# A two-block network on one NeuronCore: modulation panels as blocks, weight and row residuals moved to VectorE, retention's output weights split a head later, and gated attention in pairs of heads

## The reference

```python
def first_block(...):
    h = rms_norm(x, g_mix)
    q, k, v, su, sv, ga, gb = split(h @ w_in)
    y_att = gqa_attention(rope(q), rope(k), v) @ w_att_out     # 8 heads of 64, 2 key/value heads
    y_sgu = spatial_gating(gelu(su), gelu(sv), ...) @ w_sgu_out
    x = x + (sigmoid(ga) * y_att + sigmoid(gb) * y_sgu) @ w_out
    x = x + memory_cross_attention(rms_norm(x, g_cross), mem, w_cq, w_ckv, w_co)   # 4 heads of 128
    x = x + hierarchical_moe(rms_norm(x, g_moe), ...)
    return rms_norm(x, g_final)

def second_block(x, c, ...):
    for i in range(2):
        shift, scale, gate = split(silu(c) @ ada_w[i, 0] + ada_b[i, 0])
        h = x * (1 + scale) + shift
        y = stick_breaking_attention(h, ...) if i == 0 else retention(h, ...)
        x = layer_norm(4 ** 0.25 * x + (1 + gate) * y)
        shift, scale, gate = split(silu(c) @ ada_w[i, 1] + ada_b[i, 1])
        y = grouped_moe(x * (1 + scale) + shift, ...)
        x = layer_norm(4 ** 0.25 * x + (1 + gate) * y)
    return x
```

## Time and profile before

| | us |
|---|---|
| median of 3 runs | 1493.07 |
| lowest, highest | 1492.53, 1499.2 |
| the profiled execution | 1499.87 |
| its span, first to last instruction | 1498.0 |
| mean granted clock of TensorE | 0.975 of full |

### The profile page before, as it was taken

One profiled execution on the slowest core, in us unless ns is written; L12 is line 12 of the kernel. 1 busy time (PEld: TensorE's weight loads), 2 busy tenths in 40 slices (PEclk: granted clock), 3 DMA queues, 4 the chain that ended last, 5 costly groups with the idle time before them and its releaser, 6 DMA issues.

```text
span 1498.0 us, 22670 instructions
## 1 busy us (share of the span) xinstructions
PE 1385.2 (92%) x8222; PEld 862.5 (58%) x8223; DVE 616.9 (41%) x1323; ACT 454.1 (30%) x786; POOL 426.5 (28%) x197
## 2 busy tenths in 40 slices
PE   7999988899999989997899999899998979999985
PEld 6886776544444488775344444498876844444432
DVE  5598444522122243446233333477015254333324
ACT  4554433212121245543111111245435321112101
POOL 6892743100000077051000000279845610000000
PEclk9999999999999999999999999999998989999998
DMA  7664567699999974419699999795525499999951
GB/s 282 221 191 170 184 225 280 276 426 428 428 429 429 410 282 175 170 57 384 248 384 425 430 428 427 276 342 178 204 78 225 138 376 425 385 427 427 428 202 54
DMA packets 89597, 447.62 MB, mean 299 GB/s; under 512 B 7804, under 2 KB 9768, under 8 KB 70952
## 3 DMA queue, kind: packets, MB, share of 16 engines
q1 hardware_dynamic: 85856, 445.87, 74.8%
q10 hardware_dynamic: 3656, 0.57, 0.3%
HBM read 445.38 MB, written 1.05 MB: 298 GB/s over the span
## 4 chain that ended last, share of the span: by engine, by line
PE 66%; DMA 12%; DVE 10%; POOL 5%; issue 3%; ACT 3%; SPq 0%; DVEq 0%; ACTq 0%; POOLq 0%
PE ps L415 62%; DMA ring_hi<-in_w_up 9%; POOL WLO L2383 4%; PE ps L828 1%; PE ps L868 1%; DMA ring_lo<-in_w_co 1%; ACT WHI L1257 1%; PE ps L849 1%; DVE Z L1846 1%; DVE Z L1834 1%; DVE Z L1847 1%; DVE Z L1845 1%; DMA ring_lo<-in_w_ckv 1%; POOL RS L2352 1%; DMA ring_lo<-in_w_out 1%
## 5 line engine op out<-in xcount | busy, mean ns | idle before, releaser
L2383 POOL TENSOR_TENSOR WLO<-ring_lo,WHI 128x1024 fp32r<-128x1024 f32 (+1 forms) x158 | 386.8, 2470 | 686.5 <-ACT WHI L1257 684.7
L415 PE MATMUL ps<-ring_hi,Z 128*64 128x512 f32 x1248 | 280.1, 598 | 8.1 <-DVE Z L2082 3.0
L415 PE MATMUL ps<-ring_lo,Z 128*64 128x512 f32 x1152 | 261.4, 603 | 6.3 <-issue 5.2
L1257 ACT ACTIVATE WHI<-ring_lo 128x1024 fp32r<-128x1024 f32 (+1 forms) x160 | 165.3, 1048 | 217.5 <-PE ps L415 179.7
L415 PEld LDWEIGHTS ps<-ring_hi,Z 128*64 128x64 f32 x1248 | 90.1, 137 | 175.1 <-issue 168.7
L415 PEld LDWEIGHTS ps<-ring_lo,Z 128*64 128x64 f32 x1152 | 83.1, 139 | 159.6 <-issue 159.1
L2085 DVE TENSOR_TENSOR Z<-ps,Z 64x512 f32<-64x512 f32 x50 | 34.7, 694 | 305.1 <-ACT Z L1446 303.3
L415 PE MATMUL ps<-WHI,HTH 128*128 128x512 f32 x320 | 126.9, 397 | 8.9 <-POOL WLO L2383 5.0
L2352 POOL TENSOR_TENSOR RS<-MS,NEGH 128x1 f32<-128x1 f32 (+2 forms) x26 | 22.3, 857 | 370.2 <-DVE MS L1683 309.7
L1446 ACT ACTIVATE Z<-ps 64x512 f32<-64x512 f32 x50 | 29.5, 590 | 322.1 <-PE ps L415 322.1
L415 PE MATMUL ps<-WHI,HTL 128*128 128x512 f32 x320 | 125.2, 391 | 0.0
(11 more groups left out here) (293 smaller groups left out, 1950.3 us busy)
## 6 DMA issues: line engine op xcount, KB each, us to landing
ring_lo<-in_ada_w SPq DMA_DIRECT2D x22, 2048.0 KB, 9.1
ring_lo<-in_moe_w_gate SPq DMA_DIRECT2D x16, 2048.0 KB, 10.3
ring_lo<-in_moe_w_up SPq DMA_DIRECT2D x16, 2048.0 KB, 14.7
ring_lo<-in_moe_w_down SPq DMA_DIRECT2D x16, 2048.0 KB, 13.8
ring_hi<-in_moe_w_gate SPq DMA_DIRECT2D x16, 2048.0 KB, 11.0
ring_hi<-in_moe_w_up SPq DMA_DIRECT2D x16, 2048.0 KB, 15.5
ring_hi<-in_moe_w_down SPq DMA_DIRECT2D x16, 2048.0 KB, 12.8
ring_lo<-in_ret_w_in SPq DMA_DIRECT2D x12, 2048.0 KB, 8.0
```

What stands on the lines that cost most here:

```text
L415: return nc.tensor.matmul(o, l, r, start=start, stop=stop, skip_group_check=True)
L1257: nc.scalar.activation(WHI[:, q, 0:size], slot(r)[:, q * size:(q + 1) * size], Copy).then_inc(S("hi_split"), 1)
L2383: nc.gpsimd.tensor_tensor(WLO[:, q, 0:size], slot(r)[:, q * size:(q + 1) * size], WHI[:, q, 0:size].bitcast(F32), ALU.subtract).then_inc(S ...
```

## The change

Five parts:

1. **Modulation panels.** Panels 6 and 7 leave the cross attention; they are done as one block (`ada_block`, 8 chunks of four groups) behind `co`, panels 8 and 9 as one block in the first routing. Panels 8 and 9 are loaded into `ring_hi`, so all later panels of `ring_lo` take another slot.
2. **Lows on VectorE.** Quarters 0 and 2 of `w_out` 0, quarter 0 of `sb` 2, quarter 0 of `ret` 1, and in all three routings the low of the second half of the token rows. In `sb` and `ret` the low stands ahead of `carry` in VectorE's program.
3. **Retention.** The split of `ret_out` 0 and GpSimd's part in it move one head later; panels 20 and 21 are done in two heads instead of three.
4. **Gated attention in pairs of heads.** Scores of two heads are alternated on the two row halves, values on the two output halves; four heads' scores come ahead; the high of the values moves from VectorE to ScalarE.
5. ScalarE's wait for `x_ready` in the stick-breaking stage moves behind the split of `sb` 2.

In the diff unchanged lines are mostly left out, and a hunk that only shifts `sv_high` by 8.

```diff
@@ -264,7 +264,7 @@
                  ("ret", 0): (18, 19), ("ret", 10): (20,), ("ret", 11): (21,), ("ret_out", 3): (22, 23)}
-    IN_HIGH = {("ada", 16): 3, ("ada", 17): 4}
+    IN_HIGH = {("ada", 8): 3, ("ada", 9): 4, ("ada", 16): 3, ("ada", 17): 4}
@@ -302,7 +302,7 @@
     split_keys = list(split_no)
-    ON_VECTOR = [(("in", "sv"), 0), (("in", "sv"), 1)]
+    ON_VECTOR = [(("in", "sv"), 0), (("in", "sv"), 1), (("w_out", 0), 0), (("w_out", 0), 2), (("sb", 2), 0), (("ret", 1), 0)]
@@ -584,10 +584,10 @@
-        def ada_chunks(n):
+        def ada_chunks(n, pool="A"):
-            o = claim(pe, ("ada", n), "A")
+            o = claim(pe, ("ada", n), pool)
@@ -597,6 +597,11 @@
+        def ada_block(n):
+            chunk = ada_chunks(n, "B")
+            for c in range(KC):
+                chunk(c)
@@ -693,8 +698,44 @@
-        attention("g", 8, lambda h: GQT[half_rows(h), h // 2, :], lambda h: GKT[half_rows(h), h // 4, :],
-                  lambda h, c: GV[:, c, 64 * (h // 4):64 * (h // 4) + 64], True, {0: 0})
+        def pair_scores(j):
+            heads = (2 * j, 2 * j + 1)
+            o = [claim(pe, ("g", "s", h), "B") for h in heads]
+            for t in range(NT):
+                for k, h in enumerate(heads):
+                    ins = mm(o[k][:, t * SEQ:(t + 1) * SEQ], GQT[half_rows(h), j, t * P:(t + 1) * P], GKT[half_rows(h), j // 2, :], t == 0, t == NT - 1)
+                    if t == NT - 1:
+                        fill(ins, ("g", "s", h))
+        def head_turn(h):
+            pe.wait_ge(S("g_probs"), h + 1)
+            o = claim(pe, ("g", "p", h), "B")
+            for c in range(2):
+                for t in range(NT):
+                    ins = nc.tensor.transpose(o[:, c * SEQ + t * P:c * SEQ + (t + 1) * P], prob_buf["g"][h % 2][:, t, c * P:(c + 1) * P], ident)
+            fill(ins, ("g", "p", h))
+        def pair_values(j):
+            heads = (2 * j, 2 * j + 1)
+            for h in heads:
+                read(pe, ("g", "p", h))
+            o = [claim(pe, ("g", "v", h), "A") for h in heads]
+            v = slice(64 * (j // 2), 64 * (j // 2) + 64)
+            for c in range(2):
+                for k, h in enumerate(heads):
+                    ins = mm(o[k][half_rows(h), 0:SEQ], GV[:, c, v], probT_buf["g"][h % 2][:, c * SEQ:(c + 1) * SEQ], c == 0, c == 1)
+                    if c:
+                        fill(ins, ("g", "v", h))
+        pair_scores(0)
+        pair_scores(1)
+        ada_panel(0, "A")
+        for j in range(4):
+            head_turn(2 * j)
+            head_turn(2 * j + 1)
+            if j < 2:
+                pair_scores(j + 2)
+            pair_values(j)
@@ -734,9 +775,9 @@
         attention("c", 4, lambda h: CQT[:, h, :], lambda h: MKT[:, h, :],
-                  lambda h, c: MVV[:, c, h * P:(h + 1) * P], False, {0: 6, 4: 7})
+                  lambda h, c: MVV[:, c, h * P:(h + 1) * P], False, {})
         out_project("co", 1, 0, lambda c: read(pe, ("c", "v", c)))
-        ada_panels_now(8)
+        ada_block(6)
@@ -788,7 +829,7 @@
             if L == 0:
-                ada_panel(9)
+                ada_block(8)
@@ -811,11 +852,13 @@
-            def gather_pair():
+            def gather_pair(first=False):
                         for x in (XHR, XLR):
+                            if first and x is XLR and h == 0:
+                                pe.wait_ge(S(("rows_low", "row_1_low")[t]), L + 1)
@@ -950,9 +993,9 @@
-            pe.wait_ge(S("rows_low"), NT * (L + 1))
+            pe.wait_ge(S("rows_high"), NT * (L + 1))
             wait_pair(pe, L, "sel", 1)
-            gather_pair()
+            gather_pair(True)
@@ -1096,7 +1139,7 @@
                     ret_scores(h + 2)
-                for c in ((0, 1, 2), (3, 4, 5), (6, 7))[h] if h < 3 else ():
+                for c in range(4 * h, 4 * h + 4) if h < 2 else ():
@@ -1388,7 +1431,36 @@
-        attention("g", 8, ATT_SCALE, {0: 0})
+        def head_exps(h):
+            act.wait_ge(S("g_max"), h + 1)
+            if h >= 2:
+                result(act, ("g", "p", h - 2))
+            o = result(act, ("g", "s", h))
+            for t in range(NT):
+                ins = nc.scalar.activation(prob_buf["g"][h % 2][:, t, :], o[:, t * SEQ:(t + 1) * SEQ], ACT.Exp,
+                                           bias=SX[:, h % 2, 0, t:t + 1], scale=ATT_SCALE, accum_out=SX[:, h % 2, 1, t:t + 1])
+            drain(ins, ("g", "s", h))
+        def head_high(h):
+            o = result(act, ("g", "v", h))
+            r = slice(64 * (h % 2), 64 * (h % 2) + 64)
+            nc.scalar.activation(HTH[r, h // 2, :], o[r, 0:SEQ], Copy).then_inc(S("sv_high"), 1)
+        head_exps(0)
+        head_exps(1)
+        ada_copy(0)
+        for j in range(4):
+            for h in (2 * j, 2 * j + 1):
+                if h + 2 < 8:
+                    head_exps(h + 2)
+                if h >= 2:
+                    result(act, ("g", "v", h - 2))
+                move(("g", "p", h), probT_buf["g"][h % 2])
+            if j:
+                head_high(2 * j - 2)
+                head_high(2 * j - 1)
+        head_high(6)
+        head_high(7)
@@ -1402,8 +1474,8 @@
             move((("cq", 0), f), halves(CQT[:, 2 * f:2 * f + 2, :]))
-        attention("c", 4, X_SCALE, {0: 6, 4: 7}, ("co", 0))
-        ada_copy(8)
+        attention("c", 4, X_SCALE, {}, ("co", 0))
+        ada_copy_both(6)
@@ -1422,8 +1494,10 @@
                 nc.scalar.activation(RT[:, 128:160], RT[:, 128:160], ACT.Exp).then_inc(S("group_exp"), 1)
-            if L < 2:
-                ada_copy((9, 16)[L])
+            if L == 0:
+                ada_copy_both(8)
+            if L == 1:
+                ada_copy(16)
@@ -1515,7 +1589,6 @@
             ada_copy(11)
-            act.wait_ge(S("x_ready"), 1)
@@ -1537,6 +1610,7 @@
             split_next(("sb", 2))
+            act.wait_ge(S("x_ready"), 1)
@@ -1609,12 +1683,12 @@
                 ins.then_inc(S("ret_scaled"), 1)
-                if h == 2:
+                if h == 1:
                     turn_split("ro", 2 * h, 0, h - 1)
-                if 2 <= h < 6:
-                    split_next(("ret_out", 0), parts=(h - 2,))
+                if 3 <= h < 7:
+                    split_next(("ret_out", 0), parts=(h - 3,))
@@ -1903,7 +1977,37 @@
-        attention("g", 8, ATT_SCALE, lambda h: (half_rows(h), h // 2))
+        def head_maxima(h):
+            o = result(dve, ("g", "s", h))
+            link(V.tensor_reduce(SX[:, h % 2, 0, :], o.rearrange("p (t k) -> p t k", t=NT), AX, ALU.max))
+            V.tensor_scalar(SX[:, h % 2, 0, :], SX[:, h % 2, 0, :], -ATT_SCALE, None, ALU.mult).then_inc(S("g_max"), 1)
+        def head_normal(h):
+            read(dve, ("g", "s", h))
+            link(V.reciprocal(SX[:, h % 2, 2, :], SX[:, h % 2, 1, :]))
+            for t in range(NT):
+                pr = prob_buf["g"][h % 2][:, t, :]
+                ins = V.tensor_scalar(pr, pr, SX[:, h % 2, 2, t:t + 1], None, ALU.mult)
+            ins.then_inc(S("g_probs"), 1)
+        def head_low(h):
+            dve.wait_ge(S("sv_high"), h + 1)
+            o = result(dve, ("g", "v", h))
+            r = half_rows(h)
+            drain(V.tensor_tensor(HTL[r, h // 2, :], o[r, 0:SEQ], HTH[r, h // 2, :].bitcast(F32), ALU.subtract), ("g", "v", h))
+        head_maxima(0)
+        head_maxima(1)
+        for j in range(4):
+            for h in (2 * j, 2 * j + 1):
+                head_normal(h)
+                if h + 2 < 8:
+                    head_maxima(h + 2)
+            if j:
+                head_low(2 * j - 2)
+                head_low(2 * j - 1)
+        head_low(6)
+        head_low(7)
@@ -1926,6 +2030,7 @@
                 drain(V.tensor_tensor(g, o, g, ALU.add), ("sgu_out", "o", t, h))
+            split_low(("w_out", 0), (2 * t,))
@@ -1944,7 +2049,6 @@
         dve.wait_ge(S("small_in"), 16 * 9)
-        ada_sum(6)
@@ -2132,8 +2236,11 @@
             choose_pair(0)
-            if L < 2:
-                ada_add((8, 16)[L])
+            dve.wait_ge(S("rows_high"), NT * L + 2)
+            V.tensor_tensor(XLR[1].rearrange("p (c i) -> p c i", c=KC), XN[:, 1, :].rearrange("p (i c) -> p c i", c=KC),
+                            XHR[1].bitcast(F32).rearrange("p (c i) -> p c i", c=KC), ALU.subtract).then_inc(S("row_1_low"), 1)
+            for n in ((6, 8), (16,), ())[L]:
+                ada_add(n)
@@ -2233,6 +2340,7 @@
             turn_split("sbx", KC)
+            split_low(("sb", 2), (0,))
@@ -2276,6 +2384,7 @@
             turn_split("rx", KC)
+            split_low(("ret", 1), (0,))
@@ -2389,10 +2498,9 @@
             pool.wait_ge(S("xn_ready"), NT * (4, 5, 7)[L])
-            for t in range(NT):
-                pool.wait_ge(S("rows_high"), NT * L + t + 1)
-                nc.gpsimd.tensor_tensor(XLR[t].rearrange("p (c i) -> p c i", c=KC), src[:, t, :].rearrange("p (i c) -> p c i", c=KC),
```

(8 more changed lines are left out.)

2 lines of the change are left out of this document (1 added, 1 removed).

## The result

| | before | after |
|---|---|---|
| median of 20 runs, us | 1498.47 | 1503.17 |
| lowest to highest | 1492.53 to 1504.47 | 1498.58 to 1506.22 |
| profiled execution, its span | 1499.87, 1498.0 | 1503.08, 1501.3 |
| ratio, 95% interval | | 1.0034 [1.0022, 1.0047] |

The change makes the kernel 0.34% slower. The interval leaves out 1, so the difference is real, and it is less than the 0.5% that the prediction called no change. With 20 runs the kernel before has a median of 1498.47, not the 1493.07 of the three runs shown ahead of the prediction.

A forecast was written before the change was run, and what follows sets the result against it. TensorE, busy 92% of the span, was taken as the bound, so time counts only where it waits or runs at half clock. Terms summed to +4.45: 1493.07 + 4.45 = 1497.5 us, range 1490 to 1503.

The forecast's parts named there:

- rival B: Paired gated attention: TensorE's idling halves its clock, 6.3 us more than the forecast, 1503.8 us; chance 0.22.
- Retention projections, +10.0: Retention projections: VectorE's low ahead of `carry` makes it meet GpSimd's lows, stalling TensorE before the third panel; +10.0 us.
- Rival A: Retention projections: carry and rope don't wait turn by turn for GpSimd, so no stall; 1487.7 us, chance 0.15.
- Gated attention, +2.5: Gated attention: pairing saves TensorE time but closes a longer loop over other engines; +2.5 us, bounds −2 and +6.5.
- 2 lies between: Paired gated attention: idles of some 2 us lie between 1.64, which kept full clock, and 2.26, followed by half.
- the loop's 6.0: Gated attention: one pair's loop through ScalarE and VectorE takes 6.0 us, against 5.3 per pair before.
- Rival C: Gated attention: the loop is shorter, so pairing pays in full, −8 us; 1487.0 us, chance 0.08.
- Output weights −1.95: First block's output weights: two of four lows on VectorE let the last end earlier; −1.95 us.
- Cross attention and first experts, −2.4: Cross attention to first experts: earlier cross output and expert loads, but first expert starts no earlier; −2.4 us.
- Routings, +0.5 and −2.4: Second and third routings: row low on VectorE frees the subtraction's wait; +0.5 us in the second, −2.4 in the third.
- Retention, −1.3: Retention: output weights load some 2.2 us earlier, partly given back by later splits; −1.3 us.
- Experts, no term: Second and third experts' own stages: no change forecast, 0 us each.

The follow-up runs named there:

- Run 1: Changed kernel with the low of quarter 0 of `ret` 1 on GpSimd again, as before the change: 1493.76 us, ratio 0.9963 to the kernel before.
- run 2: Changed kernel with the low of quarter 0 of `ret` 1 still on VectorE, but behind `carry` and the modulation sum: 1493.4 us, ratio 0.9963.
- run 4: Changed kernel with useless spare products filling TensorE's idle time in the paired gated attention: 1501.31 us, ratio 1.0028 to the kernel before.
- run 10: Changed kernel with VectorE normalising both heads of a pair before taking the next pair's maxima: 1506.3 us, one execution.
- runs 5: Changed kernel with modulation panels 6 to 9 placed and loaded as before the change: 1508.55 us, ratio 1.0077 to the kernel before.
- 8: Changed kernel with attention head by head, panels as before, and the `ret` and `sb` lows behind `carry`: 1487.61 us, ratio 0.9939.
- 9: Changed kernel with single-head attention, panels as before, `ret` and `sb` lows behind `carry`, and panel 17 in `ring_lo`: 1486.6 us, ratio 0.9923.
- 11: Kernel before the change with only panel 17 moved into `ring_lo`: 1495.39 us, ratio 0.9981.

## Why the prediction was right or wrong

The difference lay where it was forecast: +4.7 between the medians of 20 against +4.45, and within 0.5%. The time did not: 1503.17 against 1497.5 is just outside the forecast's own 1490 to 1503 and next to rival B's 1503.8. It is there because the base of three executions was 5.4 us too low; B's own sum is +10.7. The difference is right with terms that are not, and that is luck.

- **Retention projections, +10.0: right**, by its own steps. Measured +9.7; `carry` at 3.3 to 3.4 each against 3.3; the second bank's read at 1009.09 in a profile that enters the stage 2.4 later, against 1008.5; idle 9.74, released by VectorE; half clock after it. Run 1 removed it, run 2 showed that order alone makes it. Rival A falls: no operation got through.
- **Gated attention, +2.5: wrong in size; rival B is what happened.** The step that failed is the one from an idle of 1.64 that left the clock at 1.00 and one of 2.26 that was followed by 0.50 to "2 lies between", read as leaving the clock up in the likeliest case. The waits here were at most 1.29 before the first slow row, yet TensorE had been busy only 1.46 of the four microseconds 133 to 137, and 0.55 followed. B's mechanism was priced at 6.3 more, 8.8 in all; measured 7.9, of which run 4 gives 5.4 to the clock. The term's own upper bound, +6.5 with half clock, was too low. At full clock the stage is 2.5 longer than before, the forecast's size, but the loop's 6.0 is not confirmed: a pair took 5.4 (with the spare products), and the waits run through scores and maxima, a link that my chain left out (it took ScalarE's highs instead); run 10 shows that this is not the whole of it either.
- **Pairing itself** does double TensorE's rate: 0.25 us a product against 0.33 where half of the first scores overlapped anyhow, or 0.51 in the earlier trace rows. Rival C fails on the loop and the clock, not on the rate: TensorE waits for the engines that read the banks. The Trainium skill (TensorEngine Tiling (Array Packing), PSUM Bottleneck) says that tiling speeds up TensorE and not the copying out of PSUM. The trace agrees: the scores and values wait 1.29 and 2.21 for ScalarE.
- **Output weights −1.95: right** (−2.0 for the stretch that holds it).
- **Cross attention and first experts, −2.4: wrong, +0.7.** `co` came 3.3 earlier, 3.7 forecast. "The first expert starts no earlier" should have read "4.5 us later": the block waited 4.16 and then ran at half clock, 2.7 more, and the row low took 2.05, not 1.25. The experts made up 3.8. Their first loads were issued earlier (272.11 against 278.77 for the second of them), which fits the forecast that the loads bound them. In the sum `sb` began 0.7 late.
- **Routings, +0.5 and −2.4: right** in sign and nearly in size (+0.6, −1.8). The row low at 2.0 is near the bound of 2.4 that I gave.
- **Retention, −1.3: too small, −3.2.** The output weights arrive before ScalarE needs them; I counted the later splits as a loss, and they cost nothing.
- **Experts, no term: wrong.** −3.4 and −4.8 with code that did not change. The second's is two stretches at half clock fewer. The third's is a slow branch of TensorE that is gone with the new slots (runs 5, 8, 9, 11), about 3.1, and the clock.

So two misses against the change (5.4 and 3.1) met three in its favour (1.9, 3.4, 4.8). The spread between executions (11.9 us before, 7.6 after) also exceeds the whole effect, so that no single execution could have confirmed the total.

## What to carry to other kernels

Before moving a two-input SBUF operation to VectorE, list what stands behind it in its program, and where GpSimd's next chain begins: the operation may be cheap and everything behind it three times as slow. A reordering that makes TensorE faster in a stage bound by others buys idle time, and idle time can halve its clock: compare the whole stage, and test with spare products. When panels are assigned to slots in rotation, a panel more or fewer early on changes when loads start in stages far behind; compare load issue times there too. And before a wait in front of a weight is called a late load, look up when the weight landed and what the engine's own sequencer did: the branch was 4.35 us of it here.
